# Decode attention over a paged cache: pages as 8 KB pieces into every fourth partition, and key products with the heads in the inner loop

## What is computed

```python
k_past = cache_k[l, page_table].reshape(bs, past, N_HEADS, 2, QK_HEAD)
v_past = cache_v[l, page_table].reshape(bs, past, N_HEADS, V_HEAD)
k_all = jnp.concatenate([k_past.astype(k.dtype), k], axis=1)
v_all = jnp.concatenate([v_past.astype(v.dtype), v], axis=1)
o = diff_attend(q, q_pos_s, k_all, v_all, k_pos_s, lam)
```

```python
s = jnp.einsum('bqhcd,bkhcd->bhcqk', q, k).astype(jnp.float32) * (QK_HEAD ** -0.5)
p = jax.nn.softmax(s, axis=-1)
a = p[:, :, 0] - lam * p[:, :, 1]
return jnp.einsum('bhqk,bkhd->bqhd', a, v.astype(jnp.float32))
```

## Time and profile before

| What | us |
|---|---|
| median of 3 runs | 2340.68 |
| the runs | 2329.11 to 2342.39 |
| the profiled execution's own time | 2342.74 |
| its span, first to last instruction | 2341.0 |
| TensorE busy in it | 1945.9 |
| VectorE busy in it | 1055.1 |
| granted TensorE clock, mean over the span | 0.912 of full |

### The profile page before, as it was taken

The page is one execution under the profiler, slowest core; times in us unless marked ns, Lnnn a source line. Parts: engine busy times, 40 slices in busy tenths (PEclk is TensorE's granted clock), DMA queues, the critical chain, the costliest instruction groups (busy, mean ns, idle before and its releaser), DMA issues.

```text
span 2341.0 us, 47863 instructions
## 1 busy us (share of the span) xinstructions
PE 1945.9 (83%) x17492; PEld 1626.3 (69%) x17492; DVE 1055.1 (45%) x1528; ACT 485.4 (21%) x831; POOL 354.1 (15%) x544
## 2 busy tenths in 40 slices
PE   5799999577686878687786597699999999799992
PEld 2378899456575767576575496577777777799991
DVE  2324221566665666567663356411111111365567
ACT  0300121021212121221212203112111211244342
POOL 0000000122332324242242101700000000000003
PEclk7799999798997989798897698799999999899996
DMA  9711122688897989798897611012121211521112
GB/s 310 258 36 36 44 100 90 237 268 287 317 346 274 377 292 386 264 386 289 313 369 261 245 37 36 18 55 89 54 72 54 90 54 54 194 99 42 41 42 92
DMA packets 210968, 404.21 MB, mean 173 GB/s; under 512 B 24426, under 2 KB 88938, under 8 KB 210788
## 3 DMA queue, kind: packets, MB, share of 16 engines
q1 hardware_dynamic: 161012, 261.51, 32.2%
q0 software_dynamic: 41488, 136.35, 15.8%
q10 hardware_dynamic: 8320, 4.19, 0.6%
HBM read 377.53 MB, written 24.51 MB: 172 GB/s over the span
## 4 chain that ended last, share of the span: by engine, by line
PE 63%; DVE 13%; DMA 8%; SPq 8%; issue 6%; ACT 1%; DVEq 0%; POOL 0%; POOLq 0%; ACTq 0%
PE psum L755 27%; PE psum L1004 11%; PE psum L763 10%; PE psum L854 5%; SPq L446 4%; DVE k_turned L1437 4%; SPq L450 3%; DMA ada_w<-w_ada 3%; DMA k_ring<-cache_k 3%; PE psum L864 2%; DVE p_t L425 2%; PE psum L738 2%; DMA v_ring<-cache_v 1%; DVE x_lo L1287 1%; PE psum L834 1%
## 5 line engine op out<-in xcount | busy, mean ns | idle before, releaser
L854 PE MATMUL psum<-k_turned,q_blocks 128*32 128x128 f32 x4096 | 333.2, 286 | 86.2 <-DVE k_turned L1437 85.7
L854 PEld LDWEIGHTS psum<-k_turned,q_blocks 128*32 128x32 f32 x4096 | 292.4, 114 | 137.8 <-issue 99.2
L1437 DVE STREAM_TRANSPOSE k_turned<-k_ring 128x2048 f32<-128x2048 f32 x128 | 295.4, 2308 | 7.6 <-DMA k_ring<-cache_k 5.0
L755 PE MATMUL psum<-x_hi,w_hi 128*128 128x512 f32 x896 | 282.0, 396 | 0.0
L755 PE MATMUL psum<-x_lo,w_hi 128*128 128x512 f32 x896 | 277.7, 391 | 0.0
L755 PE MATMUL psum<-x_hi,w_lo 128*128 128x512 f32 x896 | 276.7, 390 | 0.0
L1306 DVE TENSOR_TENSOR w_lo<-w_raw,w_hi 128x2048 fp32r<-128x2048 f32 x37 | 86.9, 2350 | 363.4 <-ACT w_hi L1062 353.7
L1004 PE MATMUL psum<-d_hi,h_hi 128*128 128x256 f32 x704 | 203.1, 289 | 12.8 <-DVE d_lo L1651 12.7
L864 PE MATMUL psum<-v_ring,p_t 128*32 128x128 f32 x4096 | 191.5, 294 | 20.3 <-DMA v_ring<-cache_v 20.1
L1004 PE MATMUL psum<-d_lo,h_hi 128*128 128x256 f32 x704 | 200.5, 285 | 0.0
L1004 PE MATMUL psum<-d_hi,h_lo 128*128 128x256 f32 x704 | 200.4, 285 | 0.0
(11 more groups left out here) (228 smaller groups left out, 2486.0 us busy)
## 6 DMA issues: line engine op xcount, KB each, us to landing
k_ring<-cache_k SPq DMA_DIRECT2D x256, 256.0 KB, 8.3
k_ring<-cache_k POOLq DMA_DIRECT2D x256, 256.0 KB, 6.2
v_ring<-cache_v SPq DMA_DIRECT2D x256, 256.0 KB, 9.2
v_ring<-cache_v POOLq DMA_DIRECT2D x256, 256.0 KB, 6.1
ada_w<-w_ada SPq DMA_DIRECT2D x12, 2048.0 KB, 9.6
w_raw<-w_in SPq DMA_DIRECT2D x12, 1024.0 KB, 5.4
w_raw<-w_gate SPq DMA_DIRECT2D x11, 1024.0 KB, 5.4
w_raw<-w_up SPq DMA_DIRECT2D x11, 1024.0 KB, 6.2
```

What stands on the lines that cost most here:

```text
L755: last = mm(psum[:, 2 * ft + c, 0:CH], w[:, s, k, ft * P:(ft + 1) * P], x[:, k, c * CH:(c + 1) * CH], start=k == 0 and j == 0, stop=k == K ...
L854: last = mm(psum[QUAD * h:QUAD * (h + 1), g % 2, 0:GP * QUAD], q_blocks[:, h, d, :], k_turned[:, g % 2, :, h * HD + d * QUAD:h * HD + (d + ...
L1437: v.transpose(k_turned[:, g % 2].rearrange("p j n -> p (j n)"), k_ring[:, g].rearrange("p j n -> p (j n)")).then_inc(k_free, 1)
```

## The change

The loop over heads is moved inside the loop over the blocks d, in `new_keys` and in `key_group`: successive products write successive quadrants, and the four products that add up in one quadrant stand four apart. The load of a page goes into every fourth partition (j, j + 4, ...), 32 in all, and each of them takes four successive tokens, 8 KB in one piece; the four pages of a group fill the 128 partitions. Before, a page went into all 128 partitions, 2 KB each. Shapes of tiles, counts, waits and all other instructions stay. Partition and slot now mean another token than before, for keys and values alike, so that `p_t` and `v_ring` still agree.

```diff
-    assert z.MODS * D // BANK == 2 * z.MODS
+    assert z.MODS * D // BANK == 2 * z.MODS and z.PAGE == QUAD * GP
...
-                    eng.dma_start(ring[:, g, j, :], pages[ds(page, 1)].rearrange("o p d -> p (o d)")
-                                  ).then_inc(landed[g], 16)
+                    eng.dma_start(ring[j::GP, g].rearrange("p i d -> p (i d)"),
+                                  pages[ds(page, 1)].rearrange("o (p i) d -> (o p) (i d)", i=GP)).then_inc(landed[g], 16)
...
             def new_keys(b):
...
-                for h in range(H):
-                    for d in range(4):
+                for d in range(4):
+                    for h in range(H):
                         last = mm(psum[QUAD * h:QUAD * (h + 1), MISC, 416:416 + QUAD], q_blocks[:, h, d, :],
...
             def key_group(b, r, g):
...
-                for h in range(H):
-                    for d in range(4):
+                for d in range(4):
+                    for h in range(H):
                         last = mm(psum[QUAD * h:QUAD * (h + 1), g % 2, 0:GP * QUAD], q_blocks[:, h, d, :],
```

## The result

The changed kernel takes 2310.66 us, median of 4 runs (2306.83 to 2312.41), against 2339.41 for the kernel before measured beside it: ratio 0.9874, 95% interval 0.9855 to 0.9894. It is faster by 29 us where 75 were forecast. Its profiled execution took 2311.05 us, span 2309.4, so 31.6 us less span than before.

What follows compares the result with a forecast made beforehand. Decode attention's engine chain was taken as the bound, the page stream near its limit, both equal after the change; 64 (seven steps) + 10 (first) + 1.5 (tail) = 75 us, 2342.7 - 75 = 2267 us, range 2225 to 2450.

Steps and rivals of the forecast that it cites:

- Part (1): Heads inside in the decode attention's key products: 2.4 us a round, 9.6 us a step, 77 us over eight steps.
- its model: A key group was to take a value group's time, 1.47 us instead of 2.68, 1.2 us less.
- Part (2): Page loads as 8 KB pieces: a quarter of the descriptors, issue rate unmoved, stream at 405 GB/s instead of 386.
- Part (3): Stream's time per decode attention step: 95 us at 405 GB/s, chain 94.4; booked 95.4, 64 us over seven steps.
- The 33.3 us of the prediction: Time from one step's last key transpose to the end of the next's first, filling at most 8.39 MB; some 31 after.
- The first step: Decode attention's step with keys alone, 93.91 us: slack in DMA, so it gets the full 10 us.
- rival C: Nothing measurable: thinner work lets TensorE's clock fall and eats the gain; chance 0.11.
- The last sequence: Tail of the decode attention: values come as fast as loaded, twelve groups 0.13 us less each, 1.5 us.
- A: Rival: the stream stays at 386 GB/s and bounds every step at 98 us; 55 us gained, 2288; chance 0.12.
- B: Rival: page loads into 32 partitions halve each other's DMA rate; 2460 at 290 GB/s, about 2770 at 200; chance 0.27.
- The row of the bias load at 210 GB/s: Trace row of a load into 32 neighbouring partitions, 24 KB pieces, engines busy at 0.93; cited for possible half rate.
- the likeliest case: The forecast itself: 75 us less over the whole kernel, 2267 us, own range 2230 to 2305; chance 0.50.

Runs made afterwards that it cites:

- heads_only: The changed kernel with its page loads taken back to 2 KB pieces over 128 partitions, heads still inside: 2322.43 us, ratio 0.9937.
- hoist_busy: The changed kernel with SyncE's pages in 2 KB pieces, the next sequence's first key transpose moved into the softmax, two dummy products a round: 2270.86 us, ratio 0.9709.

## Why the prediction was right or wrong

**Part (1), the chain: right in size, its level too high.** 9.6 us a step were forecast, with the new keys 10.1, and 9.7 is the difference of the two kernels with half loads; that just two groups of four lie on the path was not tested. But the 104.5 us of a step were taken for the chain, and it is 101.7 before and 92.0 after, not 94.4. The key group became faster than its model (1.08 us at full clock, not 1.47); over the step at its lower clock it is 21.3 us for 16 groups, 1.33 each:

```profile
L864 PE MATMUL psum<-v_ring,p_t 128*32 128x128 f32 x512 | 21.7, 323 | 5.6 <-DMA v_ring<-cache_v 5.6
L854 PE MATMUL psum<-k_turned,q_blocks 128*32 128x128 f32 x512 | 21.3, 318 | 16.6 <-DVE k_turned L1437 16.5
```

These are the groups of the step from 833.5 to 938.8 us and answer to the earlier trace rows.

**Part (2), the rate: near by luck; the issue: wrong.** 405 GB/s were taken for what the pieces allow, 401 stand in the fullest stretch after and 395 in the rounds of the six steps. That is near the 384 of SyncE's pace; what the 8 KB pieces would allow without it, no run shows. Packets fell as counted on SyncE's queue, 49152 fewer, but on GpSimd's by 16384, a third of the count (the earlier trace rows and the page after), since its packets held 3.3 KB in the mean before, more than one piece of 2 KB:

```profile
q1 hardware_dynamic: 111860, 261.51, 31.6%
q0 software_dynamic: 25104, 136.35, 15.4%
```

The sentence that failed is "Instructions and waits on SyncE and GpSimd stay one for one, so their issue rate does not move". The instructions stay, but one of them costs 0.473 us for 0.333. At 64 pages a step that is 9 us of SyncE's queue; with its old pieces the whole kernel gained 10 to 13 us, so the stream, which bounds next, would have kept most of it anyway.

**Part (3), the stream's time per step: the step that cost most.** "At 386 GB/s that is 31 + 65 = 96 us and some 2 for latency, 98; at 405 ... 95" lets the stream run at full rate from the first transpose on. It does not: after each softmax it has 14 us at about 265 GB/s, and this stood in the trace of before, though no row was read there. 14 us at 265 instead of 386 GB/s lose 4.4 us, at 253 instead of 401 5.2. With that the sum gives 102.4 and 100, and 103.2 (`heads_only`) and 100.6 (the change) were measured. That they agree so well is partly luck, as the stretches between the transposes (L1437) show, in the mean of the six steps:

| | before | `heads_only` | the change |
|---|---|---|---|
| border, last transpose to the next step's first, us | 28.4 | 28.3 | 28.3 |
| the 14 us behind it, GB/s | 253 | 270 | 262 |
| from there to the end of the last transpose, us | 62.1 | 60.9 | 58.3 |
| the same, GB/s | 384 | 385 | 395 |

The 33.3 us of the prediction are the border of the longest step, and the 31 with the edits did not come: the border kept its 28.3. The rounds were to bring 25.2 MB in 64 us and brought 26.7 in 72.3, because the border brought 7.4 MB and not the 8.39 of full rings. So the sum had the border 2.7 us too long and the rounds 8.3 too short. With SyncE's old pieces a step is still 597.7 / 6 = 99.6 us, where 95.4 were booked. So of the chain's 9.7 us a step only 104.5 - 100.6 = 3.9 came through: 23.6 instead of 54.6 us over six steps. That the two bounds came out "equal within a microsecond" should have been read as a warning: the one that is drawn too short decides.

**The first step: wrong.** "The first step has slack in DMA and gets the full 10": it got 1.3. The granted clock fell from 0.92 to 0.68 there; with dummy products it was 0.80 and the step 6.0 us shorter. That is rival C, whose evidence against it was just this step's clock before the change. Its sign, clock rows at 0.5 in the middle of a step, is seen in the later steps, too (from 864 to 868 us, for one), but there a better clock gave back only 3.2 us in six steps.

**The last sequence: wrong.** 10.6 us were booked and 0.1 came. Its chain hangs on the value pages as SyncE issues them: faster pieces, slower issue. With SyncE's old pieces it was 4.2 us shorter, with the dummy products 2.6.

**The rivals.** A was right that the pages bound each step and wrong about why: the rate did rise, and the restart and SyncE's issue held the step. B does not occur. Transfers into 32 partitions at a stride of four run at 401 GB/s with a DMA share of 1.00, and on SyncE's queue a page of keys lands in 5.2 us (median) where 8.3 were usual. The row of the bias load at 210 GB/s says nothing about this layout; that is what the Trainium skill says in SBUF — State Buffer, section Door 1: The DMA port swizzle, by which every fourth partition reaches all ports, and this trace agrees with its 401 GB/s. The row is no clean measure of the bias load either: nearly all packets that the trace counts in these 2 us are smaller than any piece of it:

```profile
DMA packets 352, 0.42 MB, mean 210 GB/s; under 512 B 335, under 2 KB 335, under 8 KB 335
```

The Trainium skill, DMA: Bandwidth & Descriptors, section Rules for kernel authors, asks for 128 partitions for full bandwidth; this trace differs, and 32 with 8 KB pieces gave more than 128 with 2 KB did (401 GB/s for 386). What 32 partitions did cost is the 0.14 us of issue on SyncE.

The measured time lies inside the whole range and above the 2305 us at which the likeliest case's own range ended.

## What to carry to other kernels

When two bounds of a loop come out equal, shortening one gains only what the other leaves: work out the second bound with all its pauses and restarts, best by reading the transfer rate in slices of some microseconds over one whole period, not from its best stretch. Before the shape of a DMA is changed, look at what its issue costs on the queue that issues it; a load in fewer pieces need not be cheaper to issue (0.473 us for 0.333 here). And work taken off TensorE where it was busy can come back as a lower clock, as in the first step here (0.92 to 0.68), where only 2.1 us went into waiting for pages.

## What the runs showed of the hardware that was not expected

- SyncE issues a page load into 128 partitions in 0.333 us, into 64 (4 KB pieces) in 0.475 and into 32 (8 KB pieces) in 0.473; GpSimd's, 0.537 for 128, takes 0.521 for 32.
- Key groups of sixteen products, neighbours in different quadrants, take 1.08 us at full clock, where four successive ones into the same quadrant made it 2.13. A value group that stood alone took 1.08 before, too; the 1.47 that the prediction set as its aim was the mean of a step at a granted clock of 0.86.
- Two products of 512 columns a round, whose result nobody uses, raised the clock granted in the first step from 0.68 to 0.80 (and in `hoist_busy` from 0.68 to 0.87) and made the kernel about 10 us faster.
